# Every eighth value unit of the sample attention is weighted and added by VectorE instead of being multiplied by TensorE

## The chip, the cores and the metric

One core of a Trainium2 chip runs the whole layer in one launch. The metric is the device time of that launch in microseconds (us); less is better. The kernel before was timed in three runs.

## The reference: what is computed

One decoder layer is applied to a prompt of 256 tokens and to 8 sample sequences of 4 new tokens each, which share all weights: normalisation, a wide input projection, a sparse attention and a short gated convolution side by side, a gated merge, an output projection, and an MLP. The change touches the last step of the sample attention. Each of the 32 sample tokens attends, with 8 heads of width 128, to the 256 past positions that an indexer picked for it (or to new positions among them):

```python
p = jax.nn.softmax(logits, axis=-1)
out = jnp.einsum('bthk,btkhd->bthd', p, v_sel.astype(jnp.float32))
```

So for every token n and head h, `out[n, h, :]` is the sum over the token's selected rows k of `p[n, h, k] * v[k, h, :]`, in float32. New values, one row per partition, take part in the same way with weights of their own, which are zero in effect where they were not selected.

## The kernel before, in words

All 288 tokens (256 prompt and 32 sample) go through the projections together. The weights of `w_in` are streamed as 44 **pairs** (NPAIR) of 256 output columns; a pair is 8 **chunks** of 128x512 numbers. For every chunk ScalarE makes a rounded high part VH (`highs`), GpSimd or VectorE makes the remainder VL (`lows`), and TensorE does 12 products (`win_half`: high by high, high by the input's low part, low by high; L428 to L430). `dve_low` says which remainders VectorE makes: in pairs 30 to 37 (VP to VP+7) those of the odd chunks. VH and VL have four slots each, so ScalarE can split chunk u only when TensorE has used chunk u-4.

The attention of the sample tokens lies between these chunks. The 64 selected rows (UNITS) are handled in **units**: unit v holds, on 128 partitions, 4 positions for each of the 32 tokens. GpSimd gathers its values, 128 rows of 1024 floats (8 heads of 128), into one of five slots of `kv` (`gather`, L1742), when the unit that used the slot is done. The weights of all units lie in `lg[:, v, h]`. To sum a unit, VectorE spreads its weights into a 128x(8x32) matrix `sp` (`spread_unit`, L1515: the constant mask `s32`, which is one where the partition belongs to token n, times the weight), and TensorE multiplies it by the rows of each head, 8 small products of 32 output rows, each of which leaves two records in the trace (`unit_sum`, L799), all of them added in PSUM bank 6. `sp` has two buffers, so the weights of unit v can be spread when the sum before the one before it, in the order of the sums, is done (`unit_summed`). TensorE does the units two at a time, v-1 and v, behind chunks j = 1, 3, 5 and 7 of pairs 30 to 37; VectorE makes the spreads at steps c = 0, 2, 4 and 6 of the same pairs. The new values (`vnrep`, 128x1024) are summed like a unit, first of all, behind chunk 0 of pair 30.

VectorE's order in these pairs is written out by hand: spreads, a remainder (L1215), and then what else the step holds: in pair 30 the top-64 search of the prompt's scores (`prompt_top`, L1416 and L1417) and the mask made of it (L1573, L1575), in pairs 31 and 32 the convolution (`conv_tile`, L1553 to L1557, L1584), and from pair 31 on, in step 1 the logits of one prompt head (`prompt_row`, L1527 to L1534), in step 5 the scaling of its probabilities (`prompt_scale`). An engine works in the order of its program; a wait holds back all that is behind it.

```python
if j % 2 and v < UNITS:
    v_unit(v - 1)
    v_unit(v)
```

Of the kernel before, what the change touches and what calls it, by code (L numbers as in the profile page):

```python
# [5 lines left out]
ALU = mybir.AluOpType  # L6
# [5 lines left out]
AX_X = mybir.AxisListType.X  # L12

P = 128
# [4 lines left out]
NS = DB * DT  # L19
TOK = SEQ + NS  # L20
H, HD = 8, 128
# [24 lines left out]
RK = 5  # L46
# [18 lines left out]
AP0 = VP + 1  # L65
NEWKEY = 35
RAW = 3
PICK = 1
XT_PIECES = ((0, 2), (2, 4), (4, 8), (8, 12), (12, 16))


def unit_end(n):
    return 8 * KP + (3 + 19 * n // 5) // 2


def dve_low(u):
# [41 lines left out]
def build(nc, I, O):  # L118
    with ExitStack() as ctx:
# [143 lines left out]
        def const(name, rows=P):  # L263
            where, t = (CP, cp) if name in CP else (CE, ce)
            a, n = where[name]
            return t[0:rows, a:a + n]
# [13 lines left out]
            "pscore_done pscore_relu pscore_acc kp_turned kp_copied sscore_done sscore_relu scomb_done scomb_added "  # L280
            "nat_done nat_copied k_vn_out kn_out comb_ready spread_done pads_zero "
            "plog_done plog_read pmax_ready pexp_done pprob_ready pt_turned pt_copied po_done po_copied "
            "unit_read conv_done tmax_ready tmax_turned tmax_wide tmax_back lg_shifted lg_exp lsum_ready lsum_wide "
            "sp_ready unit_summed o_copied ot_done ot_copied "
            "ul_ready ul_turned ul_copied u_out res_add relu_raw y_turned y_copied y_squared ssy_sum root_ready y_out "
            "ptT_in ptT_ready prow_sum prow_ready wh_ready wl_ready xh_ready xl_ready yh_ready yl_ready mix_sum dve_step "
            "xs_in x1_in sq_sum sq_made ident_in x_back hh_ready hl_ready vh_ready").split()}
# [5 lines left out]
        scratch = nc.dram_tensor("bias_scratch", [H, P * (TW + 1)], F32, kind="Internal").ap()  # L293

        NPAIR = 4 * len(SEGS) + 16
        UNIT = 8
        C_MIX = UNIT * NPAIR
        C_WO = C_MIX + 16
        C_MLP = C_WO + 16
# [104 lines left out]
        def _(pe):  # L404
            def bank(i, a=0, n=512, rows=P, r0=0):
                return PM[r0:r0 + rows, i, a:a + n]

            def transpose(out, in_):
                n = in_.shape[0]
                return pe.transpose(out, in_, cp[0:n, 0:n])  # L410
# [368 lines left out]
            def tops(j):  # L779
                if j == 3:  # L780
                    pe.wait_ge(S["ul_copied"], 2)
                    pe.wait_ge(S["tmax_ready"], 1)
                    transpose(bank(4, 0, P, H), small[:, 0:H]).then_inc(S["tmax_turned"], 1)

            def sums(j):
                if j == 0:
                    pe.wait_ge(S["tmax_wide"], 1)
                    transpose(bank(7, 0, H), smx).then_inc(S["tmax_back"], 1)
                elif j == 3:
                    pe.wait_ge(S["lsum_ready"], 1)  # L790
                    pe.matmul(bank(5, 0, H), const("b4"), small[:, 16:16 + H], start=True, stop=True).then_inc(S["lsum_wide"], 1)

            win_half(VP - 1, 0, tops)
            win_half(VP - 1, 1, sums)

            def unit_sum(ring, rows, first=False):
                for h in range(H):
                    q, c = NS * (h % 4), h // 4 * HD
                    m = pe.matmul(PM[q:q + NS, 6, c:c + HD], sp[:, ring, h, :], rows[:, h * HD:h * HD + HD],  # L799
                                  start=(first and h < 4), stop=False, skip_group_check=True)  # L800
                m.then_inc(S["unit_summed"], 1)

            def v_unit(v):
                n = UNITS + v
                pe.wait_ge(S["sp_ready"], v + 2)
                pe.wait_ge(ks[n % RK], 16 * (n // RK + 1))
                unit_sum((1 + v) % 2, kv[:, n % RK, :])

            def values_at(p, half):
                def after(j):  # L810
                    v = UNIT * (p - VP) + 4 * half + j
                    if v == 0:
                        pe.wait_ge(S["sp_ready"], 1)
                        unit_sum(0, vnrep[:], True)
                    if j % 2 and v < UNITS:
                        v_unit(v - 1)
                        v_unit(v)
                return after

            for p in range(VP, AP0 + H + 1):  # L820
# [39 lines left out]
        def _(act):  # L860
# [237 lines left out]
            for p in range(VP, AP0 + H + 1):  # L1098
                h = p - AP0
                if p == VP + UNITS // UNIT:  # L1100
                    highs(UNIT * p + 5)
                    act.wait_ge(S["unit_summed"], UNITS + 1)
                    copy(osb, bank(6, 0, 2 * P)).then_inc(S["o_copied"], 1)
                if 0 <= h < H:
                    highs(UNIT * p + 6)
                    prompt_exp(h)
                if 0 < h <= H:
                    highs(UNIT * p + 8)
                    prompt_turned(h - 1)
                if 32 <= p < 36:  # L1110
                    highs(UNIT * p + 12)
                    act.wait_ge(S["conv_done"], p - 31)
                elif p >= 39:
                    highs(UNIT * p + 12)
# [82 lines left out]
        def _(dve):  # L1197
# [299 lines left out]
            step(dve.scalar_tensor_tensor(out=past, in0=past, scalar=QKS, in1=lgb, op0=ALU.mult, op1=ALU.add))  # L1497
            step(dve.tensor_tensor(past, past, row.unsqueeze(2).to_broadcast([P, UNITS, H]), ALU.add))
            byh = lg[:].rearrange("p u h -> p h u")
            dve.tensor_reduce(small[:, 0:H], byh, AX_X, ALU.max).then_inc(S["tmax_ready"], 1)  # L1500
            lows(UNIT * (VP - 1) + 4)
            dve.wait_ge(S["tmax_turned"], 1)
            step(dve.tensor_reduce(smt, bank(4, 0, P, H).rearrange("p (n s) -> p n s", s=4), AX_X, ALU.max))
            dve.tensor_copy(smx.rearrange("p (n s) -> p n s", s=4), smt.unsqueeze(2).to_broadcast([H, NS, 4])).then_inc(S["tmax_wide"], 1)
            dve.wait_ge(S["tmax_back"], 1)
            dve.tensor_tensor(lg[:], lg[:], bank(7, 0, H).unsqueeze(1).to_broadcast([P, UNITS + 1, H]), ALU.subtract).then_inc(S["lg_shifted"], 1)
            lows(UNIT * (VP - 1) + 9)
            dve.wait_ge(S["lg_exp"], 1)
            dve.tensor_reduce(small[:, 16:16 + H], byh, AX_X, ALU.add).then_inc(S["lsum_ready"], 1)
            dve.wait_ge(S["lsum_wide"], 1)  # L1510
            step(dve.reciprocal(small[:, 32:32 + H], bank(5, 0, H)))
            step(dve.tensor_tensor(lg[:], lg[:], small[:, 32:32 + H].unsqueeze(1).to_broadcast([P, UNITS + 1, H]), ALU.mult))

# [2 lines left out]

            def spread_unit(v):

                if v:
                    dve.wait_ge(S["unit_summed"], v)  # L1520
                spread((1 + v) % 2, lg[:, v, :].unsqueeze(2).to_broadcast([P, H, NS]))

            def prompt_row(h):

# [35 lines left out]
            spread(0, lg[:, UNITS, :].unsqueeze(2).to_broadcast([P, H, NS]))  # L1560
            dve.wait_ge(S["bias_in"], 16)
            for p in range(VP, AP0 + H):
                for c in range(UNIT):
                    v = UNIT * (p - VP) + c
                    if c % 2 == 0 and v < UNITS:
                        spread_unit(v)
                        spread_unit(v + 1)
                    lows(UNIT * p + c + 4)
                    if p == VP:
                        if c < TOPP // 8 - 2:  # L1570
                            prompt_top(c + 2)
                        if c == UNIT - 1:
# [143 lines left out]
        def _(pool):  # L1716
# [18 lines left out]
            def gather(n):  # L1735

                src, u = ("cache_k", n) if n < UNITS else ("cache_v", n - UNITS)
                if RK <= n < UNITS + RK:
                    pool.wait_ge(S["unit_read"], n - RK + 1 + (n - RK > NEWKEY))
                elif n >= UNITS + RK:  # L1740
                    pool.wait_ge(S["unit_summed"], u - RK + 2)
                pool.indirect_dma_start(out=kv[:, n % RK, :], out_offset=None, in_=I[src],  # L1742
                                        in_offset=bass.IndirectOffsetOnAxis(ap=offs[:, u:u + 1], axis=0)).then_inc(ks[n % RK], 16)

# [134 lines left out]
```

## Time and profile before

| | |
|---|---|
| median of 3 runs | 1773.06 us (1772.83 to 1774.95) |
| the profiled execution's own time | 1776.01 us |
| its span, first to last instruction | 1774.2 us |
| TensorE matmul busy | 1735.7 us (98%) |
| VectorE / ScalarE / GpSimd busy | 1052.0 / 688.1 / 538.2 us |
| mean granted TensorE clock | 0.993 of full |
| chain that ended last | PE 80%, DVE 16% |

PE is TensorE's matmuls, PEld its weight loads, DVE VectorE, ACT ScalarE, POOL GpSimd, SP the queue that loads weights. Times on a timeline count from the span's start. Matmuls are pipelined, so their durations overlap; the distance between two starts tells what one costs. Pairs 30 to 37 lie between about 490 and 649 us. The lines of the chain and of the groups say who is busy most; where one engine waits for another is told by the idle time before an instruction, in square brackets, with the engine, tile and line that ended it.

### The profile page before, as it was taken

What the parts mean: (1) busy time and instruction counts of PE and PEld (TensorE: products, weight loads), DVE (VectorE), ACT (ScalarE), POOL (GpSimd) and SP (SyncE); (2) the same over time, 40 slices, a digit from 0 to 9 for tenths busy, and PEclk for the clock granted to TensorE, in tenths of its full rate; (3) what the DMA queues carried; (4) which work ended last, traced back from release to release, by engine and by line L of the source; (5) the groups of instructions that cost most, each with busy time, mean ns of one, the idle gap of its engine ahead of it and who ended that gap; (6) DMA issues with size and microseconds to landing.
All of it is one profiled execution on the core that took longest, in us unless ns stands there. A gap on an engine that the chain in (4) does not pass through costs nothing.

```text
span 1774.2 us, 32403 instructions
## 1 busy us (share of the span) xinstructions
PE 1735.7 (98%) x13634; PEld 1689.2 (95%) x13634; DVE 1052.0 (59%) x1193; ACT 688.1 (39%) x848; POOL 538.2 (30%) x432
## 2 busy tenths in 40 slices
PE   9899989999999999999999999999999999999997
PEld 9769989999988999999999999999999999999996
DVE  5979988799997432355446544455444554455543
ACT  5534433544444555333333333333333333233332
POOL 1627777889866668200231000000000000000001
PEclk9999999999999999999999999999999999999999
DMA  8616557989979965544454444444444444444442
GB/s 312 204 48 181 178 175 268 338 304 330 315 269 314 328 240 156 219 166 165 167 189 155 161 163 164 164 166 166 166 166 166 166 166 165 161 162 161 160 164 101
DMA packets 74512, 350.87 MB, mean 198 GB/s; under 512 B 9058, under 2 KB 11234, under 8 KB 53380
## 3 DMA queue, kind: packets, MB, share of 16 engines
q1 hardware_dynamic: 50304, 269.32, 44.7%
q0 software_dynamic: 19584, 71.31, 11.4%
q10 hardware_dynamic: 4516, 8.71, 1.3%
q8 instruction: 80, 1.31, 0.3%
q14 instruction: 28, 0.23, 0.0%
HBM read 342.86 MB, written 6.44 MB: 197 GB/s over the span
## 4 chain that ended last, share of the span: by engine, by line
PE 80%; DVE 16%; POOL 1%; issue 1%; DMA 1%; ACT 0%; POOLq 0%; ACTq 0%; DVEq 0%
PE PM L448 19%; PE PM L450 19%; PE PM L449 19%; PE PM L428 6%; PE PM L430 6%; PE PM L429 6%; DVE ix L1391 2%; DVE scw L1393 2%; DVE scw L1390 2%; PE PM L410 1%; PE PM L799 1%; DVE VL L1215 1%; DVE lg L1450 1%; DVE kv L1449 1%; DVE mask L1323 1%
## 5 line engine op out<-in xcount | busy, mean ns | idle before, releaser
L865 ACT ACTIVATE WH<-wring 128x2048 fp32r<-128x2048 f32 (+1 forms) x163 | 307.3, 1885 | 679.9 <-PE PM L450 676.1
L1601 DVE TENSOR_TENSOR WL<-wring,WH 128x2048 fp32r<-128x2048 f32 x159 | 364.6, 2293 | 341.0 <-ACT WH L865 340.9
L1732 POOL TENSOR_TENSOR VL<-wring,VH 128x512 fp32r<-128x512 f32 x274 | 358.1, 1316 | 180.3 <-ACT VH L865 175.7
L428 PE MATMUL PM<-hH,VH 128*128 128x288 f32 x1312 | 398.8, 304 | 10.0 <-POOL VL L1732 6.5
L429 PE MATMUL PM<-hL,VH 128*128 128x288 f32 x1312 | 389.1, 297 | 0.0
L430 PE MATMUL PM<-hH,VL 128*128 128x288 f32 x1312 | 387.8, 296 | 0.0
L448 PE MATMUL PM<-XH,WH 128*128 128x288 f32 x1280 | 379.1, 296 | 1.5 <-DVE WL L1608 1.5
L448 PE MATMUL PM<-YH,WH 128*128 128x288 f32 x1280 | 379.4, 296 | 0.0
L449 PE MATMUL PM<-YL,WH 128*128 128x288 f32 x1280 | 377.6, 295 | 0.0
L449 PE MATMUL PM<-XL,WH 128*128 128x288 f32 x1280 | 377.6, 295 | 0.0
L450 PE MATMUL PM<-XH,WL 128*128 128x288 f32 x1280 | 376.3, 294 | 0.0
L450 PE MATMUL PM<-YH,WL 128*128 128x288 f32 x1280 | 376.3, 294 | 0.0
L865 ACT ACTIVATE VH<-wring 128x512 fp32r<-128x512 f32 x352 | 221.6, 631 | 321.5 <-PE PM L430 296.5
L428 PEld LDWEIGHTS PM<-hH,VH 128*128 128x128 f32 x1312 | 248.0, 189 | 24.3 <-issue 14.1
L1782 POOL TENSOR_SCALAR ysam<-ysam,small 32x1024 f32<-32x1024 f32 x2 | 6.2, 3123 | 824.1 <-DVE small L1707 824.1
L430 PEld LDWEIGHTS PM<-hH,VL 128*128 128x128 f32 x1312 | 248.9, 190 | 0.0
L429 PEld LDWEIGHTS PM<-hL,VH 128*128 128x128 f32 x1312 | 248.5, 189 | 0.2
L448 PEld LDWEIGHTS PM<-XH,WH 128*128 128x128 f32 x1280 | 239.8, 187 | 1.8 <-ACT G L954 1.7
L450 PEld LDWEIGHTS PM<-XH,WL 128*128 128x128 f32 x1280 | 241.1, 188 | 0.0
L450 PEld LDWEIGHTS PM<-YH,WL 128*128 128x128 f32 x1280 | 241.1, 188 | 0.0
L449 PEld LDWEIGHTS PM<-XL,WH 128*128 128x128 f32 x1280 | 240.3, 188 | 0.1
L449 PEld LDWEIGHTS PM<-YL,WH 128*128 128x128 f32 x1280 | 240.3, 188 | 0.0
(280 smaller groups left out, 1703.1 us busy)
## 6 DMA issues: line engine op xcount, KB each, us to landing
wring<-w_in SPq DMA_DIRECT2D x176, 512.0 KB
wring<-w_mlp_in SPq DMA_DIRECT2D x64, 1024.0 KB
wring<-w_mlp_out SPq DMA_DIRECT2D x64, 1024.0 KB
wring<-w_o SPq DMA_DIRECT2D x16, 1024.0 KB
wring<-w_pb SPq DMA_DIRECT2D x8, 1024.0 KB
wring<-w_pa SPq DMA_DIRECT2D x8, 1024.0 KB
xT<-x_t SPq DMA_DIRECT2D x1, 2304.0 KB, 10.0
kv<-x_prompt SPq DMA_DIRECT2D x2, 1024.0 KB, 8.6
```

The lines of the kernel that those rows point to most:

```text
L428: pe.matmul(out, vh, th[:, k, :], start=(k == 0), stop=False)
L429: pe.matmul(out, vh, tl[:, k, :], start=False, stop=False)
L430: m = pe.matmul(out, vl, th[:, k, :], start=False, stop=(k == KT - 1))
L448: pe.matmul(out, wh, rh[:, k0 + k, :], start=(first and k == 0), stop=False)
L449: pe.matmul(out, wh, rl_[:, k0 + k, :], start=False, stop=False)
L450: m = pe.matmul(out, wl, rh[:, k0 + k, :], start=False, stop=(last and k == CK - 1))
L865: return act.activation(out, in_, ACT.Copy, **kw)
L1390: step(dve.max(v8, sc2))
L1391: step(dve.max_index(ix[:, 8 * i:8 * i + 8], v8, sc2))
L1393: step(dve.match_replace(sc2, v8, sc2, MARK))
L1601: dve.tensor_tensor(WL[:, i % 2], wring[:, i % 2], WH[:, i % 2], ALU.subtract).then_inc(S["wl_ready"], 1)
L1732: pool.tensor_tensor(VL[:, u % 4], r, VH[:, u % 4], ALU.subtract).then_inc(S["vl_pool"], 1)
```

## The change: what it does

Of each eight units the last (7, 15, ... 63; `dve_unit`) is no longer spread and multiplied. VectorE instead multiplies its gathered rows by the weights and adds them to `vnrep`, head by head, in 8 operations on 128x128 (`add_unit`), at step 7 of each of the pairs 30 to 37. So that this works, `vnrep` is first multiplied by the new values' weights in one operation on 128x1024 (`new_values`), at step 0 of pair 30. At the end, behind chunk 0 of pair 38, TensorE multiplies `vnrep` by the constant mask `s32`, which sums the rows of each token: 8 small products. The product of the new values behind chunk 0 of pair 30, and its spread, are gone. The count of spreads becomes `summed(v)`. GpSimd, before it gathers into a slot that held such a unit, waits for VectorE's sum instead of TensorE's. Six semaphores of the softmax become two (`soft_ready`, `soft_turned`), which count the same events in the same order.

```diff
+def dve_unit(v):
+    return v % UNIT == UNIT - 1
+def summed(v):
+    return sum(not dve_unit(w) for w in range(v))
...
             def v_unit(v):
-                n = UNITS + v
-                pe.wait_ge(S["sp_ready"], v + 2)
+                n, i = UNITS + v, summed(v)
+                pe.wait_ge(S["sp_ready"], i + 1)
                 pe.wait_ge(ks[n % RK], 16 * (n // RK + 1))
-                unit_sum((1 + v) % 2, kv[:, n % RK, :])
+                unit_sum(lambda h: sp[:, i % 2, h, :], kv[:, n % RK, :], v == 0)
...
-                    if v == 0:
-                        pe.wait_ge(S["sp_ready"], 1)
-                        unit_sum(0, vnrep[:], True)
                     if j % 2 and v < UNITS:
-                        v_unit(v - 1)
-                        v_unit(v)
+                        for w in (v - 1, v):
+                            if not dve_unit(w):
+                                v_unit(w)
+                    elif v == UNITS:
+                        pe.wait_ge(S["unit_added"], UNITS // UNIT + 1)
+                        unit_sum(lambda h: const("s32"), vnrep)
...
             def spread_unit(v):
-                if v:
-                    dve.wait_ge(S["unit_summed"], v)
-                spread((1 + v) % 2, lg[:, v, :].unsqueeze(2).to_broadcast([P, H, NS]))
+                i = summed(v)
+                if i >= 2:
+                    dve.wait_ge(S["unit_summed"], i - 1)
+                spread(i % 2, lg[:, v, :].unsqueeze(2).to_broadcast([P, H, NS]))
+            def add_unit(v):
+                n = UNITS + v
+                dve.wait_ge(ks[n % RK], 16 * (n // RK + 1))
+                dve.wait_ge(S["unit_added"], v // UNIT + 1)
+                for h in range(H):
+                    c = slice(HD * h, HD * h + HD)
+                    m = dve.scalar_tensor_tensor(out=vnrep[:, c], in0=kv[:, n % RK, c], scalar=lg[:, v, h:h + 1], in1=vnrep[:, c],
+                                                 op0=ALU.mult, op1=ALU.add)
+                m.then_inc(S["unit_added"], 1)
+            def new_values():
+                dve.wait_ge(S["nat_copied"], 16)
+                byhead = vnrep[:].rearrange("p (h d) -> p h d", h=H)
+                dve.tensor_tensor(byhead, byhead, lg[:, UNITS, :].unsqueeze(2).to_broadcast([P, H, HD]), ALU.mult).then_inc(S["unit_added"], 1)
...
                     if c % 2 == 0 and v < UNITS:
-                        spread_unit(v)
-                        spread_unit(v + 1)
+                        for w in (v, v + 1):
+                            if not dve_unit(w):
+                                spread_unit(w)
                     lows(UNIT * p + c + 4)
+                    if v == 0:
+                        new_values()
+                    elif v < UNITS and dve_unit(v):
+                        add_unit(v)
...
                 elif n >= UNITS + RK:
-                    pool.wait_ge(S["unit_summed"], u - RK + 2)
+                    if dve_unit(u - RK):
+                        pool.wait_ge(S["unit_added"], (u - RK) // UNIT + 2)
+                    else:
+                        pool.wait_ge(S["unit_summed"], summed(u - RK) + 1)
```

How the order of instructions moves is shown at three places. The first is VectorE at the start of pair 30 (step 0). Before, the first spread is that of the new values, the next two are units 0 and 1; the `VL` rows are remainders of chunks 1 and 3 of the pair, `mask` the prompt's scores:

```order
L1515 TENSOR_TENSOR sp<-cp,lg 128x256 [waits ul_turned,dve_step]
L1515 TENSOR_TENSOR sp<-cp,lg 128x256 [waits bias_in]
L1515 TENSOR_TENSOR sp<-cp,lg 128x256 [waits unit_summed]
L1215 TENSOR_TENSOR VL<-wring,VH 128x512 [waits vh_ready] x2
L1416 MAX m8p<-mask_62 128x8
```

and with the change:

```order
L1524 TENSOR_TENSOR sp<-cp,lg 128x256 [waits bias_in,ul_turned,dve_step]
L1524 TENSOR_TENSOR sp<-cp,lg 128x256
L1224 TENSOR_TENSOR VL<-wring,VH 128x512 [waits vh_ready] x2
L1548 TENSOR_TENSOR vnrep<-vnrep,lg 128x1024 [waits nat_copied]
L1425 MAX m8p<-mask_62 128x8
```

One spread is gone, and the wait for TensorE's sum of the new values with it; the 128x1024 product is new, behind the two remainders.

The second place is VectorE at steps 6 and 7 of pair 30 and step 0 of pair 31 (units 6, 7, 8 and 9). Before:

```order
L1515 TENSOR_TENSOR sp<-cp,lg 128x256 [waits unit_summed,dve_step]
L1515 TENSOR_TENSOR sp<-cp,lg 128x256 [waits unit_summed]
L1215 TENSOR_TENSOR VL<-wring,VH 128x512 [waits vh_ready]
L1573 TENSOR_SCALAR mask_62<-mask_62 128x384
L1575 TENSOR_TENSOR mask_62<-mask_62,later 128x128 [waits dve_step] x2
```

and with the change:

```order
L1524 TENSOR_TENSOR sp<-cp,lg 128x256 [waits unit_summed,dve_step]
L1224 TENSOR_TENSOR VL<-wring,VH 128x512 [waits vh_ready]
L1540 SCALAR_TENSOR_TENSOR vnrep<-kv,lg,vnrep 128x128 [waits unit_added,rows_in1]
L1540 SCALAR_TENSOR_TENSOR vnrep<-kv,lg,vnrep 128x128 x7
L1604 TENSOR_SCALAR mask_62<-mask_62 128x384
L1606 TENSOR_TENSOR mask_62<-mask_62,later 128x128 [waits dve_step] x2
```

One spread has gone and eight operations have come, behind the remainder and ahead of the rest of step 7 and of the spreads of units 8 and 9.

The third place is TensorE behind chunk 7 of pair 30, where units 6 and 7 were summed; L760 and L761 are the logits of the first prompt head. Before:

```order
L430 MATMUL PM<-hH,VL 128x288
L799 MATMUL PM<-kv,sp 32x128 [waits rows_in0,sp_ready]
L799 MATMUL PM<-kv,sp 32x128 x7
L799 MATMUL PM<-kv,sp 32x128 [waits rows_in1,sp_ready]
L799 MATMUL PM<-kv,sp 32x128 x7
L760 MATMUL PM<-kT,qT 128x128
```

and with the change:

```order
L438 MATMUL PM<-hH,VL 128x288
L807 MATMUL PM<-kv,sp 32x128 [waits rows_in0,sp_ready]
L807 MATMUL PM<-kv,sp 32x128 x7
L768 MATMUL PM<-kT,qT 128x128
L769 MATMUL PM<-kT,qT 128x256
```

Eight products are gone there, as behind the last chunk of each pair up to 37.

## Rows read from the trace of the kernel before

**Rows 1.** The page's first part: busy time, share of span, instructions of each engine.

```profile
PE 1735.7 (98%) x13634; PEld 1689.2 (95%) x13634; DVE 1052.0 (59%) x1193; ACT 688.1 (39%) x848; POOL 538.2 (30%) x432
```

**Rows 2.** Busy time by stage: stretch, length, each engine's busy us (instructions), clock, DMA.

```profile
529.30:552.30 23.00, 20.09 (x235) 18.48 (x231) 22.36 (x54) 9.69 (x17) 13.41 (x13) 0.93 0.88 302
...
571.50:590.70 19.20, 19.20 (x241) 17.66 (x235) 9.26 (x21) 10.02 (x18) 13.68 (x13) 1.00 0.90 316
```

**Rows 3.** Waits of TensorE's weight loads from 488 to 652: total us, times, longest.

```profile
PEld PM L799 <- DVE sp L1515: 5.3, 5, 2.0
```

**Rows 4.** Timeline, TensorE: start, length; a block of two units, and one unit alone.

```profile
633.67 0.29 PE L430 MATMUL PM<-hH,VL 128*128 128x288 f32 x1
633.89 0.81 PEld L799 LDWEIGHTS PM<-kv,sp 128*32 128x32 f32 x32 [0.17 <-issue]
...
634.90 0.40 PE L428 MATMUL PM<-hH,VH 128*128 128x288 f32 x1
...
504.10 0.38 PEld L799 LDWEIGHTS PM<-kv,sp 128*32 128x32 f32 x16 [0.17 <-issue]
```

**Rows 5.** Timeline at the start of pair 30: VectorE's first spreads and remainders, TensorE behind them.

```profile
491.11 0.76 DVE L1515 TENSOR_TENSOR sp<-cp,lg 128x256 f32<-128x256 f32 x2
492.42 0.43 DVE L1515 TENSOR_TENSOR sp<-cp,lg 128x256 f32<-128x256 f32 x1 [0.55 <-PE PM L799]
492.76 2.38 DVE L1215 TENSOR_TENSOR VL<-wring,VH 128x512 fp32r<-128x512 f32 x2
...
493.49 0.19 PEld L428 LDWEIGHTS PM<-hH,VH 128*128 128x128 f32 x1 [1.42 <-DVE VL L1215]
```

**Rows 6.** VectorE operations akin to the new ones: timeline rows, and a group (count, busy, mean ns).

```profile
528.98 0.48 DVE L1556 SCALAR_TENSOR_TENSOR zB<-uv,gcol,zB 128x256 f32<-128x256 f32 x1
529.38 0.25 DVE L1557 SCALAR_TENSOR_TENSOR zB<-uv,gcol,zB 128x32 f32<-128x32 f32 x1
...
513.11 0.28 DVE L1527 SCALAR_TENSOR_TENSOR scw<-PM,G 128x128 f32<-128x128 f32 x1
513.31 0.42 DVE L1529 SCALAR_TENSOR_TENSOR scw<-PM,G 128x256 f32<-128x256 f32 x1
...
L1449 DVE TENSOR_TENSOR kv<-kv,PM 128x1024 f32<-128x1024 f32 x64 | 77.5, 1211 | 3.5 <-DMA kv<-cache_k,offs 3.5
```

**Rows 7.** Timeline, pairs 31 to 33: VectorE's spreads, and TensorE's blocks behind them.

```profile
515.74 0.86 DVE L1515 TENSOR_TENSOR sp<-cp,lg 128x256 f32<-128x256 f32 x2 [0.77 <-PE PM L799]
...
544.94 0.75 DVE L1515 TENSOR_TENSOR sp<-cp,lg 128x256 f32<-128x256 f32 x2
...
545.41 1.08 PE L799 MATMUL PM<-kv,sp 128*32 128x128 f32 x32 [1.78 <-DVE sp L1515]
...
553.69 0.75 DVE L1515 TENSOR_TENSOR sp<-cp,lg 128x256 f32<-128x256 f32 x2
...
557.04 1.08 PE L799 MATMUL PM<-kv,sp 128*32 128x128 f32 x32
```

**Rows 8.** Timeline, end of pair 33 and start of 34: VectorE, and TensorE's next block.

```profile
568.02 0.68 DVE L1215 TENSOR_TENSOR VL<-wring,VH 128x512 fp32r<-128x512 f32 x1
571.25 1.32 DVE L1515 TENSOR_TENSOR sp<-cp,lg 128x256 f32<-128x256 f32 x2 [2.55 <-PE PM L799]
...
576.25 1.08 PE L799 MATMUL PM<-kv,sp 128*32 128x128 f32 x32
```

**Rows 9.** Timeline, pair 37, VectorE: the spreads of units 62 and 63.

```profile
643.70 1.85 DVE L1515 TENSOR_TENSOR sp<-cp,lg 128x256 f32<-128x256 f32 x2 [2.04 <-PE PM L799]
```

**Rows 10.** Timeline, pair 32: a remainder on GpSimd, and VectorE beside it.

```profile
550.03 1.28 POOL L1732 TENSOR_TENSOR VL<-wring,VH 128x512 fp32r<-128x512 f32 x1 [0.98 <-ACT VH L865]
...
550.05 1.41 DVE L1553 TENSOR_SCALAR zB<-uv,gcol 128x256 f32<-128x256 f32 x1
```

**Rows 11.** Busy time by stage, as in rows 2, behind the wait at 545.41.

```profile
546.40:550.60 4.20, 4.20 (x24) 4.17 (x21) 4.08 (x12) 0.64 (x1) 2.91 (x3) 0.59 0.80 235
```

More of the change, by code:

```diff
@@ L67 @@
 RAW = 3
+UNIT = 8
 PICK = 1
@@ L282, in build @@
             "plog_done plog_read pmax_ready pexp_done pprob_ready pt_turned pt_copied po_done po_copied "
-            "unit_read conv_done tmax_ready tmax_turned tmax_wide tmax_back lg_shifted lg_exp lsum_ready lsum_wide "
-            "sp_ready unit_summed o_copied ot_done ot_copied "
+            "unit_read conv_done soft_ready soft_turned lg_shifted lg_exp "
+            "sp_ready unit_summed unit_added o_copied ot_done ot_copied "
             "ul_ready ul_turned ul_copied u_out res_add relu_raw y_turned y_copied y_squared ssy_sum root_ready y_out "
@@ L295, in build @@
         NPAIR = 4 * len(SEGS) + 16
-        UNIT = 8
         C_MIX = UNIT * NPAIR
@@ L781, in tops, with unit_sum @@
                     pe.wait_ge(S["ul_copied"], 2)
-                    pe.wait_ge(S["tmax_ready"], 1)
-                    transpose(bank(4, 0, P, H), small[:, 0:H]).then_inc(S["tmax_turned"], 1)
+                    pe.wait_ge(S["soft_ready"], 1)
+                    transpose(bank(4, 0, P, H), small[:, 0:H]).then_inc(S["soft_turned"], 1)
             def sums(j):
                 if j == 0:
-                    pe.wait_ge(S["tmax_wide"], 1)
-                    transpose(bank(7, 0, H), smx).then_inc(S["tmax_back"], 1)
+                    pe.wait_ge(S["soft_ready"], 2)
+                    transpose(bank(7, 0, H), smx).then_inc(S["soft_turned"], 1)
                 elif j == 3:
-                    pe.wait_ge(S["lsum_ready"], 1)
-                    pe.matmul(bank(5, 0, H), const("b4"), small[:, 16:16 + H], start=True, stop=True).then_inc(S["lsum_wide"], 1)
+                    pe.wait_ge(S["soft_ready"], 3)
+                    pe.matmul(bank(5, 0, H), const("b4"), small[:, 16:16 + H], start=True, stop=True).then_inc(S["soft_turned"], 1)
             win_half(VP - 1, 0, tops)
             win_half(VP - 1, 1, sums)
-            def unit_sum(ring, rows, first=False):
+            def unit_sum(weights, rows, first=False):
                 for h in range(H):
                     q, c = NS * (h % 4), h // 4 * HD
-                    m = pe.matmul(PM[q:q + NS, 6, c:c + HD], sp[:, ring, h, :], rows[:, h * HD:h * HD + HD],
+                    m = pe.matmul(PM[q:q + NS, 6, c:c + HD], weights(h), rows[:, h * HD:h * HD + HD],
                                   start=(first and h < 4), stop=False, skip_group_check=True)
@@ L1101, in _ @@
                     highs(UNIT * p + 5)
-                    act.wait_ge(S["unit_summed"], UNITS + 1)
+                    act.wait_ge(S["unit_summed"], summed(UNITS) + 1)
                     copy(osb, bank(6, 0, 2 * P)).then_inc(S["o_copied"], 1)
@@ L1499, in _ @@
             byh = lg[:].rearrange("p u h -> p h u")
-            dve.tensor_reduce(small[:, 0:H], byh, AX_X, ALU.max).then_inc(S["tmax_ready"], 1)
+            dve.tensor_reduce(small[:, 0:H], byh, AX_X, ALU.max).then_inc(S["soft_ready"], 1)
             lows(UNIT * (VP - 1) + 4)
-            dve.wait_ge(S["tmax_turned"], 1)
+            dve.wait_ge(S["soft_turned"], 1)
             step(dve.tensor_reduce(smt, bank(4, 0, P, H).rearrange("p (n s) -> p n s", s=4), AX_X, ALU.max))
-            dve.tensor_copy(smx.rearrange("p (n s) -> p n s", s=4), smt.unsqueeze(2).to_broadcast([H, NS, 4])).then_inc(S["tmax_wide"], 1)
-            dve.wait_ge(S["tmax_back"], 1)
+            dve.tensor_copy(smx.rearrange("p (n s) -> p n s", s=4), smt.unsqueeze(2).to_broadcast([H, NS, 4])).then_inc(S["soft_ready"], 1)
+            dve.wait_ge(S["soft_turned"], 2)
             dve.tensor_tensor(lg[:], lg[:], bank(7, 0, H).unsqueeze(1).to_broadcast([P, UNITS + 1, H]), ALU.subtract).then_inc(S["lg_shifted"], 1)
@@ L1508, in _ @@
             dve.wait_ge(S["lg_exp"], 1)
-            dve.tensor_reduce(small[:, 16:16 + H], byh, AX_X, ALU.add).then_inc(S["lsum_ready"], 1)
-            dve.wait_ge(S["lsum_wide"], 1)
+            dve.tensor_reduce(small[:, 16:16 + H], byh, AX_X, ALU.add).then_inc(S["soft_ready"], 1)
+            dve.wait_ge(S["soft_turned"], 3)
             step(dve.reciprocal(small[:, 32:32 + H], bank(5, 0, H)))
@@ L1559, in _ @@
             dve.wait_ge(S["ul_turned"], 2)
-            spread(0, lg[:, UNITS, :].unsqueeze(2).to_broadcast([P, H, NS]))
             dve.wait_ge(S["bias_in"], 16)
```

## Prediction, made before the changed kernel ran

> **What bounds the kernel now.** I read the page's busy shares first: TensorE's matmuls fill 98% of the span, VectorE is busy for 59% [rows 1]. So a us of work taken from TensorE is worth a us, unless TensorE waits just there. Whether it does is a question of the stage, so I read the busy time by stage next. Between 529.3 and 552.3 VectorE is busy for 22.36 of 23.00 us and TensorE for only 20.09; from 571.5 to 590.7 TensorE is busy throughout and VectorE for 9.26 of 19.20 us [rows 2]. The value units lie in both kinds of stage: pairs 30 to 32, where VectorE also makes the prompt's mask and the convolution, and pairs 33 to 37, where it has time. The waits say the same: TensorE's loads wait 5.3 us in total for `sp`, in 5 places [rows 3], and on the timeline all of these are before 546; the longest idle time of the matmuls is 1.78 us, ahead of the block at 545.41, whose spreads had only begun at 544.94 [rows 7]. In pairs 30 to 32 the bound is VectorE's list, in pairs 33 to 37 TensorE.
>
> **What a unit costs TensorE.** A block of two units occupies the loads for 0.81 us, one unit for 0.38; the difference, 0.43 us, is what the second unit of a block costs [rows 4]. The change drops the second unit of 8 blocks: 8 x 0.43 = 3.4 us, if TensorE is the bound at all eight. The rest of the block (idle 0.17 ahead, a step behind) stays, since a first unit remains. The product of the new values moves from a block of its own in pair 30 to one in pair 38: from the last product before a block to the first one behind it 1.23 us pass with two units [rows 4], 0.80 with one, some 0.1 of it in any case; so 0.7 us is added at pair 38, and what is gained in pair 30 is counted by VectorE's list below.
>
> **What it costs VectorE.** An added unit is 8 operations, each with two inputs of 128x128 in SBUF. No row shows this form in these pairs. The same operation on 128x256 takes 0.48 us, and the next starts 0.40 behind it; on 128x32 it takes 0.25 [rows 6]. 128 columns lie between: about 0.35 in length and 0.27 from start to start, 8 x 0.27 = 2.15 us a unit. From below: with one input from PSUM, 128x128 starts 0.20 ahead of its successor [rows 6], 1.6 us a unit. From above: if nothing overlaps, 8 x 0.35 = 2.8. I take 2.15, since the 256-column row has the same kinds of inputs. The multiplication of the new values on 128x1024 takes 1.2 us by the nearest group of that size [rows 6]. A spread saved is worth 0.34 us (two of them take 0.76, one 0.43) [rows 5].
>
> **The sum in pairs 30 to 32.** I follow VectorE's list from the start of pair 30 to the block at 545.41, the last one that waits for it [rows 7]:
> - Start: VectorE makes one spread less and doesn't wait 0.55 us for the sum of the new values. Its remainders start at about 491.9 instead of 492.76, 0.9 us earlier [rows 5]. TensorE, which waits 1.42 us for the first of them, gains that too, but it meets the list again at the next spreads, so only the list counts.
> - The multiplication of the new values, behind the remainders: +1.2.
> - Units 7 and 15: two spreads less, -0.7, two additions more, +4.3.
> - The one wait of the list for TensorE at 515.74, 0.77 us [rows 7], is swallowed: -0.8.
>
> Together -0.9 + 1.2 - 0.7 + 4.3 - 0.8 = +3.1 us at that block. The 0.43 us that TensorE saves at units 7 and 15 is worth nothing here, as it would wait longer. Behind the block TensorE's own time runs again. The addition of unit 23 comes between the spreads of unit 22 and those of units 24 and 25: these start at 553.69 + 3.1 + 2.15 - 0.34 = 558.6, the first is ready at 559.0. TensorE comes for it at 557.04 [rows 7] + 3.1 - 0.43 = 559.7. So unit 23 is covered, by a margin of 0.7 us, and the shift is 3.1 - 0.4 = +2.7 at the start of pair 33.
>
> **Pairs 33 to 38.** Here VectorE idles 2.55 us ahead of the first spreads of the next pair, after a remainder at 568.02, and these are needed only at 576.25 [rows 8]. An addition of 2.15 us fits, and even if the gathered rows landed only when TensorE would have used them (about 571), addition and spreads would be done by 574.5. Each of the five units saves its 0.43: -2.15. At pair 38 TensorE must wait for the addition of unit 63. Its neighbours' spreads begin at 643.70 [rows 9]; the addition would end about 648, and TensorE comes for it only behind a further chunk, about 651: no wait. The mask product adds 0.7. GpSimd's new wait for an addition holds back only gathers whose rows are used a pair later, and the remainders behind them, which wait for ScalarE anyway. Prompt rows and scalings move with VectorE's list, 3 us late where their readers are half a pair away: nothing. The renamed softmax semaphores: nothing, the same events in the same order.
>
> Sum: +3.1 - 0.43 - 2.15 + 0.7 = **+1.2 us**. The span goes from 1774.2 to 1775.4, the profiled execution's own time from 1776.01 to 1777.2; the median of the runs shown lies 2.95 below that execution, so I forecast 1773.06 + 1.2 = 1774.3.
>
> **GpSimd beside VectorE.** While GpSimd makes a remainder from 550.03 on, for 1.28 us, an operation of VectorE that started 0.02 later took 1.41 us, though its kind takes 0.35 [rows 10]: it stood until GpSimd was done, a loss of 1.1. VectorE is busy without a gap in pairs 30 to 32, so nearly every remainder already meets something there, and added work changes what is met rather than how often; I take the net as zero and put two meetings more, 2.2 us, at the upper end, and one fewer, at the multiplication of the new values, which may just start ahead of GpSimd, 1.1 us at the lower.
> The Trainium skill (SBUF — State Buffer, section "SBUF: two separate sides") makes a rule of this: a VectorE operation with two SBUF inputs and a GpSimd operation take a shared pair of ports as an exclusive lock, and the loser stands for the whole instruction. By that rule each of the eight-fold additions is open to it, and it speaks against this change; the row above agrees.
>
> **The rivals.**
> - **VectorE keeps up everywhere.** TensorE gains all eight units, 3.4 us, and 0.9 at the start of pair 30: -4.3 us, 1768.8 (the move of the mask product cancels). For it: 59% busy. Against it: rows 2 and 3, and a list without a gap. It would need an addition to cost little more than the spread it replaces. 0.07.
> - **Slower: additions meet remainders, and the clock falls once more.** The place is pairs 31 and 32, steps 7, where the list is already late. Two meetings cost 2.2 us, additions at their upper price 1.3 for two units. Behind the wait at 545.41 the granted clock is 0.59 over 4.2 us, so for most of it at 1.2 GHz instead of 2.4 [rows 11], a loss of about 1.5 us in products. The waits get longer with this change (about 2.5 us, where some were below 1), so a second such stretch may come; it costs 1.5 if no wait behind it swallows it. Together 1.2 + 2.2 + 1.5 = +4.9 us, 1778.0; it decides from 2.3 us beyond my sum on, one meeting and the clock. 0.25.
> - **The two stages cancel at zero or a little below**: additions at 1.6 a unit (-1.1), the multiplication ahead of GpSimd (-1.1): -1.0 us, 1772.1. 0.2, within the bound.
> - **The change doesn't take work off TensorE.** The order shows that the eight products of the unit are gone, and the mask product comes once. Only if a first unit alone costs as much as two would 3.4 us become nothing; rows 4 speak against it. 0.03, at +3.8 us.
>
> The Trainium skill (TensorE: Matmul & The Clock Gate, section "What's actually happening") says that the gate goes by how busy the array has been lately; that is in keeping with the fall behind the wait, and would make the slower rival likelier, not the forecast other.
>
> **How the numbers follow.** A measurement of this kernel can tell about 0.2%, 3.5 us, from no change. Even the whole of TensorE's saving, 3.4 us, is less than that. My forecast, +1.2, has 0.45. Forecast and cancelling case lie within; of the slower rival's 0.25 nearly all lies above +3.5, as does half of the last one. Faster needs the first rival: 0.07. Slower 0.25, same 0.68. For the range, downward all lower prices and the fall of the clock gone (1.2 - 1.1 - 1.1 - 1.5 = -2.5), upward the upper price of two additions and two meetings (1.2 + 1.3 + 2.2 = +4.7), a little wider for what lies between runs (1772.83 to 1774.95): 1770.4 to 1778.2.
>
> **What would show it.** In the changed profile: the eight operations on `vnrep` start some 0.27 us apart, 2.15 us a unit; TensorE's waits for `sp` in pairs 31 and 32 grow from 5.3 us to 8 or 9; no wait of TensorE for `sp` from pair 33 on and none for `unit_added` at pair 38; the distance from the first block of pair 33 to the first of pair 38 is 2.15 us shorter. The block that was at 545.41 comes about 3.1 us later, if the start of pair 30 stands where it stood. The forecast is wrong if that block moves by less than 1 us (the list has more room than I found) or by more than 5 (meetings or clock).

## The result, and the profile after

| | before | changed |
|---|---|---|
| median, 12 runs each | 1773.91 us | 1779.2 us (1775.8 to 1780.89) |
| ratio | 1 | 1.0024, 95% interval 1.0016 to 1.0031 |
| the profiled execution's own time | 1776.01 us | 1775.8 us |
| its span | 1774.2 us | 1774.0 us |
| mean granted clock | 0.993 | 0.991 |

The change makes the kernel slower by 0.24%, 4.3 us by the ratio. The profiled execution is the shortest of the 12, so its own time must not be set against the median. Most of what it lacks lies ahead of the change: the first spread of pair 30 stands at 489.01, before at 491.11 [rows 5], in code that is the same in both, and in the profiles of the experiments it stands anywhere from 487.1 to 492.8. So I count all positions below from that first spread.

The page's first part, and the stages of [rows 2], of the changed kernel:

```profile
PE 1733.7 (98%) x13506; PEld 1687.5 (95%) x13506; DVE 1075.3 (61%) x1249; ACT 687.6 (39%) x848; POOL 541.7 (31%) x432
```

```profile
529.30:552.30 23.00, 20.17 (x240) 18.10 (x240) 22.47 (x52) 10.78 (x18) 14.39 (x13) 1.00 0.80 279
552.30:571.50 19.20, 17.32 (x201) 16.11 (x199) 13.34 (x35) 8.56 (x16) 11.70 (x12) 1.00 0.86 304
571.50:590.70 19.20, 19.20 (x230) 17.48 (x233) 13.29 (x30) 10.32 (x19) 15.12 (x13) 1.00 0.95 336
```

TensorE has lost 128 records and 2.0 us of busy time; VectorE has 23.3 us more. As before, VectorE is busy almost without a gap from 529 to 552 (22.47 of 23.00 us), and TensorE throughout from 571 to 590. What is new is the stage between, in which TensorE is busy for 17.32 of 19.20 us; before it was busy for all of it:

```profile
552.30:571.50 19.20, 19.20 (x239) 17.65 (x235) 10.20 (x24) 10.02 (x18) 12.81 (x12) 1.00 0.91 316
```

The waits of TensorE's weight loads for `sp` have doubled against [rows 3], from 5.3 us in 5 places to 11.2 us in 8:

```profile
PEld PM L807 <- DVE sp L1524: 11.2, 8, 2.3
```

The timeline of VectorE in the changed kernel shows its start, the addition of unit 7, and then its way from the spreads for the block at 546.57 to those for the block at 558.19, with the addition of unit 23. The second fence has GpSimd's two remainders on that way.

```profile
489.01 0.76 DVE L1524 TENSOR_TENSOR sp<-cp,lg 128x256 f32<-128x256 f32 x2
489.69 1.29 DVE L1224 TENSOR_TENSOR VL<-wring,VH 128x512 fp32r<-128x512 f32 x2
490.89 1.22 DVE L1548 TENSOR_TENSOR vnrep<-vnrep,lg 128x1024 f32<-128x1024 f32 x1
...
508.40 2.18 DVE L1540 SCALAR_TENSOR_TENSOR vnrep<-kv,lg,vnrep 128x128 f32<-128x128 f32 x8
510.50 0.35 DVE L1604 TENSOR_SCALAR mask<-mask 128x384 f32<-128x384 f32 x1
...
546.10 0.76 DVE L1524 TENSOR_TENSOR sp<-cp,lg 128x256 f32<-128x256 f32 x2
...
550.87 3.27 DVE L1540 SCALAR_TENSOR_TENSOR vnrep<-kv,lg,vnrep 128x128 f32<-128x128 f32 x8
...
555.05 0.25 DVE L1584 SCALAR_TENSOR_TENSOR zB<-uv,gcol,zB 128x32 f32<-128x32 f32 x1
...
555.74 1.26 DVE L1584 SCALAR_TENSOR_TENSOR zB<-uv,gcol,zB 128x32 f32<-128x32 f32 x1
...
557.72 0.76 DVE L1524 TENSOR_TENSOR sp<-cp,lg 128x256 f32<-128x256 f32 x2
```

```profile
551.07 1.28 POOL L1763 TENSOR_TENSOR VL<-wring,VH 128x512 fp32r<-128x512 f32 x1 [1.21 <-ACT VH L874]
...
555.52 1.44 POOL L1763 TENSOR_TENSOR VL<-wring,VH 128x512 fp32r<-128x512 f32 x1 [0.18 <-ACT VH L874]
```

An undisturbed addition takes 2.10 us from its first start to the next instruction, near the 2.15 of the forecast. That of unit 23 takes 3.27: GpSimd's remainder begins 0.2 us into it, and it loses the 1.1 us of [rows 10] again. A second remainder, at 555.52, meets an operation of the convolution 4.9 us later, which takes 1.26 us where its like took 0.25. So two remainders fall between the spreads at 546.10 and those at 557.72; before, only the one of [rows 10] fell between the spreads at 544.94 and 553.69 [rows 7]. The rule that I had set beside those rows (the Trainium skill, SBUF — State Buffer, section "SBUF: two separate sides") speaks of operations with two SBUF inputs. The one in [rows 10] has a single tensor as input; the new operation has two, and the 3.27 us beside the remainder agree with the rule.

TensorE's blocks behind it, in the changed kernel, and the product of the mask at pair 38:

```profile
546.57 1.08 PE L807 MATMUL PM<-kv,sp 128*32 128x128 f32 x32 [1.72 <-DVE sp L1524]
...
558.19 1.08 PE L807 MATMUL PM<-kv,sp 128*32 128x128 f32 x32 [1.88 <-DVE sp L1524]
...
576.95 1.08 PE L807 MATMUL PM<-kv,sp 128*32 128x128 f32 x32
...
650.41 0.65 PE L807 MATMUL PM<-vnrep,cp 128*32 128x128 f32 x16
```

The block that was at 545.41 stands at 546.57: 57.6 us behind the first spread, where it was 54.3. The first block of pair 33, at 558.19, waits 1.88 us for VectorE; in [rows 7] it waited for nothing. And from pair 33 on VectorE waits for rows:

```profile
568.33 0.69 DVE L1224 TENSOR_TENSOR VL<-wring,VH 128x512 fp32r<-128x512 f32 x1
571.16 2.16 DVE L1540 SCALAR_TENSOR_TENSOR vnrep<-kv,lg,vnrep 128x128 f32<-128x128 f32 x4 [2.15 <-DMA kv<-cache_v,offs]
```

The page's waits give 8.3 us of this in four places; no wait of TensorE follows from them, as the blocks up to the last of pair 37, at 646.75, show none.

### The profile page after: what moved, and what is told of

It is laid out like the page before. It is cut to its first block, busy times and chain, and to the rows that moved or that the text cites. A ratio compares the mean times of both kernels' runs of the same rounds, so it can differ in the third digit from the quotient of the medians.

```text
span 1774.0 us, 32203 instructions
## 1 busy us (share of the span) xinstructions
PE 1733.7 (98%) x13506; PEld 1687.5 (95%) x13506; DVE 1075.3 (61%) x1249; ACT 687.6 (39%) x848; POOL 541.7 (31%) x432
## 4 chain that ended last, share of the span: by engine, by line
PE 79%; DVE 17%; issue 1%; POOL 1%; DMA 1%; ACT 0%; POOLq 0%; ACTq 0%; DVEq 0%
PE PM L456 19%; PE PM L458 19%; PE PM L457 19%; PE PM L436 6%; PE PM L437 5%; PE PM L438 5%; DVE ix L1400 2%; DVE scw L1402 2%; DVE scw L1399 2%; PE PM L418 1%; DVE VL L1224 1%; DVE lg L1459 1%; DVE kv L1458 1%; PE PM L807 1%; DVE mask L1332 1%
```

## The experiments

Two theories were set against each other. **The list:** VectorE's hand-written list bounds pairs 30 to 32, an addition there costs its own length, an addition in pairs 33 to 37 costs nothing and saves 0.43 us. **The clock:** the longer waits bring low-clock stretches, in which TensorE runs at 1.2 GHz instead of 2.4, and these are most of the loss. All kernels but before2 were built from the changed one; in moved, early, late, late2, late2nv and late3nv, `added(v)`, the count of added units below v, replaces `v // UNIT` in the waits on `unit_added`. A block is TensorE's products of the one or two units behind a chunk. The positions in the table are from one profile each, in us behind the first spread of pair 30.

| kernel | ratio to before (95%) | first block of pair 33 | last block of pair 37 | low-clock stretches, pairs 30 to 33 |
|---|---|---|---|---|
| before, first profile | 1 | 65.9 | 156.3 | at 56 |
| before2 (one run) | | 64.2 | 154.6 | none |
| changed | 1.0024 (1.0016 to 1.0031) | 69.2 | 157.7 | at 37 |
| again | 1.0020 (1.0011 to 1.0029) | 69.2 | 159.3 | at 37, 71 |
| again2 | 1.0023 (1.0014 to 1.0032) | 68.3 | 158.4 | at 36, 70 |
| moved | 1.0008 (0.9999 to 1.0017) | 64.3 | 155.0 | none |
| early | 1.0031 (1.0019 to 1.0044) | 69.3 | 161.1 | at 37, 71 |
| late | 0.9989 (0.9980 to 0.9998) | 64.5 | 153.6 | none |
| late2 | 0.9973 (0.9961 to 0.9984) | 63.2 | 149.6 | none |
| late2nv | 0.9972 (0.9961 to 0.9983) | 63.0 | 149.5 | at 53 |
| late3nv | 0.9989 (0.9980 to 0.9998) | 63.0 | 151.8 | at 52 |
| behind | 1.0023 (1.0013 to 1.0033) | 70.1 | 158.7 | at 37, 60 |
| fill | 1.0015 (1.0006 to 1.0024) | 68.3 | 156.9 | at 36 |
| fill2 | 1.0017 (1.0007 to 1.0026) | 68.6 | 157.2 | at 48 |

**again**, the changed kernel once more.

> The changed kernel itself, unedited, to see an execution that is typical of its median. In the one profile so far its stage from the first spread of pair 30 to the first product of pair 38 took 159.5 us, 1.0 more than before, and 0.9 more passed behind it, but that execution was the shortest of 12 (1775.8, median 1779.2). Theory (VectorE's list in pairs 30 to 32 plus the moved product): the same stage shows 1 to 2 us more than before, the rest equal; ratio near 1.001. Rival (clock): the stage is longer by another 1.5 us or more, in stretches at 1.2 GHz that come behind TensorE's waits, and the mean granted clock is 0.989 to 0.991 against 0.993; ratio 1.002 to 1.003.

1779.49 us against 1775.48. Its profile is more typical than the first. The waits are the same to 0.1 us, but behind the wait in pair 33 there is now a stretch with long products. From the timeline of again, the block and the first two products behind it, and the stage:

```profile
560.60 1.58 PE L807 MATMUL PM<-kv,sp 128*32 128x128 f32 x32 [1.89 <-DVE sp L1524]
562.11 0.61 PE L436 MATMUL PM<-hH,VH 128*128 128x288 f32 x1
562.51 0.44 PE L437 MATMUL PM<-hL,VH 128*128 128x288 f32 x1
```

```profile
562.00:565.40 3.40, 3.40 (x21) 3.29 (x18) 2.46 (x7) 1.29 (x5) 1.51 (x2) 0.64 0.79 254
```

A product takes 0.44 us where it takes 0.29 at full clock, and the next block comes 5.9 us behind this one (75.2 against 69.2) where the first profile has 4.4. That is 1.5 us, and no later wait swallows it. The other stretch, at 37, costs nothing: it lies between two waits for VectorE (at 35.0 and 46.7), and the second takes it up. The two kernels fill and fill2 (below) show this, as they are alike up to pair 33: fill has that stretch (at 36), and TensorE waits 1.11 us at the block at 46.0; fill2 doesn't have it, and TensorE waits 2.89 us at the same block, at 46.2. From the first spread to the first product of pair 38 again takes 161.1 us, the first profile 159.5, before 158.5.

**before2**, the kernel before once more.

> The kernel before, unedited, for a second profile of it. The stage from the first spread of pair 30 to the first product of pair 38 took 158.5 us with one low-clock stretch (13 long products) behind the wait of 1.78 us. Both theories: the same stage within 0.2 us if the low-clock stretch is there again, 157.0 if it is not.

156.8 us, without a low-clock stretch. Its wait is 1.75 us, the one of [rows 7] 1.78, so the same wait is followed by a stretch in one execution [rows 11] and not in the other. From the timeline of before2, the block behind chunk 5 of pair 32 and the next:

```profile
545.84 1.08 PE L799 MATMUL PM<-kv,sp 128*32 128x128 f32 x32 [1.75 <-DVE sp L1515]
550.24 1.08 PE L799 MATMUL PM<-kv,sp 128*32 128x128 f32 x32
```

The next block follows in 4.40 us, in the first profile in 5.9. So a stretch is worth 1.5 us, and whether it comes is left to the execution.

**moved, early and late**: no added units; units 7, 15 and 23 alone; units 31 to 63 alone.

```diff
 def dve_unit(v):
-    return v % UNIT == UNIT - 1
+    return False                                # moved
+    return v % UNIT == UNIT - 1 and v < 24      # early
+    return v % UNIT == UNIT - 1 and v >= 24     # late
```

> No unit is added by VectorE; only the new values are weighted at the start of pair 30 and summed by the mask product at pair 38. Theory: VectorE's list starts 0.9 us earlier and is 1.2 longer, the product moves: +0.3 to +1.0 us against before (1773.3 to 1774.9). Rival (clock): TensorE's waits are as long as before, so no low-clock stretch more, the same time. Rival (the move is the whole cost): +3 us or more.

> Only units 7, 15 and 23 are added by VectorE, those of the pairs in which its list has no gap. Theory: +3.1 at the block that was at 545.41, less 0.4 for unit 23, plus 0.7 for the mask product: +3.4 us against before. Rival (clock): +5 us or more, with low-clock stretches between 510 and 560. If VectorE had room, +0.7 or less.

> Only units 31, 39, 47, 55 and 63 are added by VectorE, those of the pairs in which it idles. Theory: five times 0.43 saved, the start and the moved product cost 0.3 to 1.0: -1.2 to -1.9 us against before (about 1771.5). Rival (clock): as before it has one low-clock stretch, so the same as the theory. Rival (gathered rows come late and hold VectorE until TensorE waits): TensorE waits for sp from pair 33 on, +1 us or more.

Moved: 1777.13 us, +1.4 by the ratio, with an interval that holds zero and the theory's +0.3 to +1.0. Early: 1781.23 us, +5.5; the list alone had said +3.4, and the clock rival "+5 us or more, with low-clock stretches". Its profile has both: the block of pair 33 where the changed kernel has it (69.3), and behind it a stretch (this stage holds it):

```profile
560.00:566.00 6.00, 4.60 (x47) 4.22 (x48) 5.22 (x13) 2.56 (x7) 2.05 (x3) 0.72 0.69 224
```

Late: 1773.58 us, -2.0 by the ratio, next to the theory's -1.2 to -1.9; its waits for `sp` all lie ahead of pair 33. So the three early units cost some 4 us against moved and the five late ones gain some 3.4: the sign of the change is decided by the place of the units. These sizes are rough, as each ratio is known to about 1.6 us: five times 0.43 would be 2.2, and moved's +1.4 with both parts gives +2.1, where the changed kernel, run beside them (again), has +3.6.

**behind**, the additions of units 7, 15 and 23 a step later.

```diff
-                    elif v < UNITS and dve_unit(v):
+                    elif c == 0 and v <= UNITS and dve_unit(v - 1) and behind(v - 1):   # v - 1 < 24
+                        add_unit(v - 1)
+                    elif v < UNITS and dve_unit(v) and not behind(v):
                         add_unit(v)
```

> The additions of units 7, 15 and 23 come a step later, behind the spreads of step 0 of the next pair; the amount of work is the same. Theory (VectorE's list bounds pairs 30 to 32): units 7 and 15 gain little, unit 23 is moved to a place where VectorE idles, so the block at 69.2 us comes 2.0 us earlier, TensorE doesn't wait there, and the low-clock stretch behind it goes: 3 to 3.5 us less than with the change, near the time before. Rival (only the amount of VectorE's work counts): no more than 0.5 us less.

The rival's number came: 1778.88 us, the same as the changed kernel. TensorE no longer waits in pair 33, but it waits 3.65 us at the block at 35.4 and 3.87 at that at 58.9. In these pairs the list has no place where VectorE idles, so moving an addition moves the wait. That I expected 2 us at unit 23 was wrong: the addition of unit 15 now lies behind the first block of pair 32 instead of ahead of it, so the block that stood at 57.6 comes at 58.9, and one of the low-clock stretches (at 60) stands behind it, where no wait swallows it.

**fill and fill2**, eight products of ones ahead of TensorE's block in pair 33, so that it is busy instead of idle; nobody reads their result. In fill they are written beside the unit sums in PSUM bank 6 and disturb these, so its attention of the sample tokens is not the reference's; in fill2 they go to bank 7.

```diff
+                    if v == FILL:                       # 25
+                        pe.wait_ge(S["po_copied"], 1)   # fill2 alone
+                        for i in range(8):
+                            pe.matmul(bank(7, 0, P), ones[:], ones[:], start=True, stop=True)
```

> The changed kernel with eight products of ones by ones (128x128, their result is read by nobody, some 1.7 us) ahead of TensorE's block behind chunk 1 of pair 33, where it idles 1.9 us for sp. Clock theory (the idle time there brings the low-clock stretch behind it, 1.5 us): the block stands where it stood (69.2 us behind the first spread), the stretch behind it is gone, the time is 1.0 to 1.5 us less than with the change. Rival (the stretch has nothing to do with that wait, or the waits at 35 and 58 us bring it): the stretch stays, the time is the same or 0.3 us more.

> As fill, with the eight products of ones in a PSUM bank that is free there, so that nothing else is disturbed. Clock theory: no long products behind the block of pair 33, and 1 to 2 us less than again2. Rival (the stretch is no matter of that wait, and the first difference was chance): within 0.5 us of again2.

> The changed kernel, unedited, on the same chip as the next kernel: 1779 us or 1.002 of before. Of its profiles so far one showed a low-clock stretch behind the wait of 1.9 us in pair 33 and one did not.

The filler does what it should; from the timeline of fill2:

```profile
559.25 1.95 PE L824 MATMUL PM<-ones 128*128 128x128 f32 x16
561.40 1.08 PE L808 MATMUL PM<-kv,sp 128*32 128x128 f32 x32 [0.21 <-DVE sp L1529]
565.80 1.08 PE L808 MATMUL PM<-kv,sp 128*32 128x128 f32 x32
```

The wait is 0.21 us instead of 1.9, the block stands where it stood, and the next follows in 4.40 us: no stretch. In the profiles, a wait of 1.9 us in pair 33 was followed by one in three of four (again, again2, early; not in the first of the changed kernel), the filled one in none of two. The times don't settle it: fill is at 1.0015, but fill2 with 1778.48 us isn't below again2 on the same chip (1777.74), and the intervals overlap. The kernel late speaks against the idle time as the whole cause. Its wait in pair 32 is 2.27 us, longer than any of 1.9 us in pair 33, and no stretch follows it, as the next block comes in 4.40 us. From its timeline:

```profile
545.77 1.08 PE L811 MATMUL PM<-kv,sp 128*32 128x128 f32 x32 [2.27 <-DVE sp L1528]
550.17 1.08 PE L811 MATMUL PM<-kv,sp 128*32 128x128 f32 x32
```

So that the idle time in pair 33 brings the stretch is suggested by the profiles, and shown neither by them nor by the times.

**late2, late2nv and late3nv**: more late units, and the new values weighted later.

```diff
-    return v % UNIT == UNIT - 1
+    return v % 4 == 3 and v >= 24                   # late2, late2nv
+    return v % 8 in (3, 5, 7) and v >= 24           # late3nv
...
-                    if v == 0:
+                    if v == 24:                     # late2nv, late3nv
                         new_values()
```

> Two units of each pair from 33 on (27, 31, 35, ... 63) are added by VectorE, ten in all. Theory: another five times 0.43, so 2.15 us less than with five late units, about -4.1 us against before (0.9977). Rival (VectorE is held by rows that land late, 8.3 us in 4 places with the change, and by GpSimd's remainders): TensorE waits for sp in pairs 33 to 37, and the gain is smaller than with five, or gone.

> As late2 (ten late units), and the new values are weighted at step 0 of pair 33 instead of pair 30. Theory (list-bound start): 1.2 us come off VectorE's list in pairs 30 to 32 and the block at 53 us comes up to 1.2 us earlier: 0.5 to 1.2 us less than late2's 1769.6. Rival (the list is bound by something else, so 1.2 us there don't matter): equal to late2.

> Three units of each pair from 33 on (those with v modulo 8 of 3, 5 and 7), fifteen in all, and the new values at pair 33. If VectorE still keeps up: another 2.15 us less than late2nv. Rival: its list in pairs 33 to 37 is now without a gap (three additions, spreads, remainders, rows that land late, GpSimd's remainders), TensorE waits for sp there, and the gain stops or turns, +1 to +6 us against late2nv.

Late2: 1769.6 us, -4.8 us by the ratio (0.9973), the best together with late2nv, and faster than the kernel before and the changed one; the theory had said -4.1. From the first block of pair 33 to the last of pair 37 it takes 86.4 us, moved 90.7: 4.3 us for nine of its ten units, where nine times 0.43 are 3.9. VectorE waits 12.9 us for rows, and TensorE waits for no spread in these pairs. Late2nv gains nothing on late2 (1770.02): its list is 1.8 us earlier at the block in pair 32 (51.4 against 53.1), but in its profile a low-clock stretch stands behind that block, and at pair 33 only 0.3 is left. Whether its other executions have that stretch too isn't known. Late3nv goes back to -2.0 us: the rival's full list. From its timeline, VectorE at the end of pair 37, GpSimd's remainders beside it, and TensorE's last block but the mask's:

```profile
631.39 3.45 DVE L1544 SCALAR_TENSOR_TENSOR vnrep<-kv,lg,vnrep 128x128 f32<-128x128 f32 x8
...
635.70 6.37 DVE L1544 SCALAR_TENSOR_TENSOR vnrep<-kv,lg,vnrep 128x128 f32<-128x128 f32 x8
```

```profile
635.10 3.12 POOL L1767 TENSOR_TENSOR VL<-wring,VH 128x512 fp32r<-128x512 f32 x2 [0.41 <-ACT VH L878]
639.06 1.28 POOL L1767 TENSOR_TENSOR VL<-wring,VH 128x512 fp32r<-128x512 f32 x1 [0.85 <-ACT VH L878]
640.66 1.26 POOL L1767 TENSOR_TENSOR VL<-wring,VH 128x512 fp32r<-128x512 f32 x1 [0.32 <-ACT VH L878]
```

```profile
643.11 1.08 PE L811 MATMUL PM<-kv,sp 128*32 128x128 f32 x16 [3.26 <-DVE sp L1528]
```

One addition takes 6.37 us, three times its length, with four remainders beside it, and TensorE waits 3.26. A low-clock stretch stands behind that wait as well:

```profile
642.80:646.20 3.40, 3.09 (x23) 2.49 (x24) 2.36 (x9) 0.38 (x1) 0.00 (x0) 0.51 0.51 154
```

## Why the prediction was right in most of its steps and short in its sum

The range, 1770.4 to 1778.2, holds the ratio applied to the 1773.06 us that it started from (1777.3), though not the 12-run median (1779.2). It took 3.5 us as the least that can be told from no change and gave "same" 0.68; the measured +4.3 us (+3.6 and +4.1 in the repeats) lie just above that limit, on the side of the slower rival. Of that rival's parts one meeting with a remainder and the second low-clock stretch came; its +4.9 us had two meetings (and left out the 1.3 us for dearer additions that it names).

- **A unit costs TensorE 0.43 us: right.** Ten late units show it (late2), and moved against late: 90.7 and 89.1 us from the first block of pair 33 to the last of 37, 1.6 us for four units. In the changed kernel the way from the first block of pair 33 to the first product of pair 38 is 2.3 us shorter than before (90.3 against 92.6); 2.15 were forecast.
- **An addition costs VectorE 2.15 us: right, undisturbed 2.10.** With one remainder of GpSimd in it, that of unit 23 takes 3.3 us; with four, one of late3nv takes 6.4.
- **The list moves the block at 545.41 by 3.1 us: right.** It moved by 3.3, and by 3.4 against before2; and VectorE has no wait left ahead of it, as forecast. That VectorE bounds pairs 30 to 32 is shown by behind, early and late.
- **"So unit 23 is covered, by a margin of 0.7 us": wrong.** TensorE waits 1.88 us there. Two things undid the margin. The first is a meeting that I had put at net zero. From the spreads for the one block to those for the next VectorE takes 11.62 us (546.10 to 557.72), before 8.75 (544.94 to 553.69): 2.87 more, where an addition less a spread is 1.8. The rest, 1.1 us, is one remainder more that falls into the longer list. It isn't decisive whether the addition itself is met. In again2 it isn't, the convolution is met twice instead, and TensorE waits 1.86 us all the same. From its timeline:

```profile
551.14 1.27 DVE L1584 SCALAR_TENSOR_TENSOR zB<-uv,gcol,zB 128x32 f32<-128x32 f32 x1
552.45 2.22 DVE L1540 SCALAR_TENSOR_TENSOR vnrep<-kv,lg,vnrep 128x128 f32<-128x128 f32 x8
...
556.28 1.26 DVE L1584 SCALAR_TENSOR_TENSOR zB<-uv,gcol,zB 128x32 f32<-128x32 f32 x1
```

  The second is that I had carried along the low-clock stretch behind 545.41, which held TensorE back by 1.5 us in that one execution. In the changed kernel that place had no such stretch, so TensorE came earlier and waited. The block of pair 33 is 3.3 us later than in the first profile of before and 4.9 later than in the second; the forecast was +2.7. That it lies so near the 3.3 is luck: a stretch that was gone (-1.5) against a wait that was not foreseen (+1.9).
- **The clock put into a rival and not into the sum: the term that was missing.** A stretch behind the new wait costs 1.5 us and was there in three of four profiles with that wait. Ledger of again: +2.6 us at the first product of pair 38, and 1125.6 us from there to the end where before has 1124.6, +1.0 for the mask product (0.7 forecast): +3.6, its measured ratio. The first profile, without the stretch in pair 33, gives 1.0 + 0.9 = +1.9 in the same way. It is near the forecast of +1.2 by the luck just told. Both are set against a profile of before with a stretch; against before2, which has none, again has +5.2 and the first profile +3.5. So the measured 3.6 to 4.3 us lie within what the profiles give. How many executions of each kernel have which stretch isn't known, so the ledger fits them and doesn't prove them.
- **Late rows harmless: right** for one and two units a pair, but for 0.29 us that TensorE waits once in late for rows. **No wait at pair 38: right** within 0.2 us (again shows 0.19).
- **"Even the whole of TensorE's saving, 3.4 us, is less than that": too cautious** about what can be told from no change. With the 12 runs of the changed kernel the interval is 0.08% to either side, 1.4 us, so +0.24% and even the -0.11% of late stand clear of zero.

What stays open is what decides about the stretches: the idle time alone doesn't, since executions with equal waits differ and a wait of 2.27 us had none.

## What to carry to other kernels

Work moved to an engine that is idle on average belongs in the stretches where it is idle, pair by pair: here the same edit is worth -0.11% with five late units, -0.27% with ten, and +0.31% with three early ones; with fifteen late units VectorE's list was full there too, and it was back at -0.11%. Where a hand-written list has no gap, moving the work along it moves the wait. And a margin that rests on a slow stretch in one execution is no margin; take a second profile of the kernel before.

## What had not been expected of the hardware

Low-clock stretches of TensorE come in one execution and not in another at the same wait: 1.78 us of idle time with one behind it, 1.75 and even 2.27 without. The one in pair 33 of again (granted clock 0.64 over 3.40 us) lengthens a product from 0.29 to 0.44 us and costs 1.5 us; one that is followed by a wait for another engine is taken up by it (fill against fill2). And eight small operations of VectorE can take three times their length (6.37 us for 2.1) when four operations of GpSimd fall beside them. A longer list also meets more of these, wherever in it they fall.
